# Both mixers of the first block reordered: first table load, second weight tile, filler products, tile rests and masks

## The reference

```python
def mla_mixer(h, w_dq, q_norm, w_uq, w_dkv, kv_norm, w_ukv, q_gain, k_gain, w_o):
    cq = rms_norm(h @ w_dq, q_norm)
    q = (cq @ w_uq).reshape(b, s, MLA_HEADS, MLA_QK)
    dkv = h @ w_dkv
    ckv = rms_norm(dkv[..., :MLA_KV_RANK], kv_norm)
    k_rope = jnp.broadcast_to(dkv[..., None, MLA_KV_RANK:], (b, s, MLA_HEADS, MLA_ROPE))
    kv = (ckv @ w_ukv).reshape(b, s, MLA_HEADS, MLA_NOPE + MLA_V)
    ...
    q = rms_norm(q, q_gain)
    k = rms_norm(k, k_gain)
    ...
    o = chunk_causal_attention(q, k, v)
    return o.reshape(b, s, MLA_HEADS * MLA_V) @ w_o

def mlstm_mixer(h, w_in, w_if, b_if, head_norm, w_o):
    q, k, v, o_pre = jnp.split(h @ w_in, [hq, 2 * hq, 2 * hq + hv], axis=-1)
    ...
        dmat = bcum[..., :, None] - bcum[..., None, :] + li[..., None, :]
        dmat = jnp.where(causal, dmat, -jnp.inf)
        m_t = jnp.maximum(inter, jnp.max(dmat, axis=-1))
        w_intra = jnp.exp(dmat - m_t[..., None])
        qk = jnp.einsum('bhtd,bhsd->bhts', qc, kc) * w_intra
        ...
        hc = num / jnp.maximum(jnp.abs(den), jnp.exp(-m_t))[..., None]
```

## Time and profile before

| | us |
|---|---|
| time, median of three runs | 1621.61 |
| the three runs | 1624.91, 1621.61, 1619.29 |
| profiled execution, time | 1625.26 |
| its span, first to last instruction | 1623.4 |
| TensorE busy | 1585.5 (98%) |
| VectorE busy | 1076.5 (66%) |
| ScalarE busy | 863.8 (53%) |
| GpSimd busy | 151.3 (9%) |
| mean granted TensorE clock | 0.986 of full |

### The profile page before, as it was taken

One profiled execution on the slowest core, in us unless ns is written; L12 is line 12 of the kernel. 1 busy time (PEld: TensorE's weight loads), 2 busy tenths in 40 slices (PEclk: granted clock), 3 DMA queues, 4 the chain that ended last, 5 costly groups with the idle time before them and its releaser, 6 DMA issues.

```text
span 1623.4 us, 33219 instructions
## 1 busy us (share of the span) xinstructions
PE 1585.5 (98%) x11604; PEld 1492.1 (92%) x11604; DVE 1076.5 (66%) x1817; ACT 863.8 (53%) x1381; POOL 151.3 (9%) x133
## 2 busy tenths in 40 slices
PE   7899999999999999999999999999999999999999
PEld 6789998877999889999899999889999878999997
DVE  6668766645677666666787766678566755686665
ACT  5576554444765545445545545556455546664443
POOL 1650000075200000000000000000000032200000
PEclk8899999989999999999999999999999999999999
DMA  6226556543565565555655655556555871065564
GB/s 227 73 56 192 193 182 193 183 155 117 168 190 186 182 196 188 185 183 192 204 188 182 197 189 188 188 181 207 179 190 193 216 198 65 2 195 189 186 195 142
DMA packets 80766, 280.72 MB, mean 173 GB/s; under 512 B 8880, under 2 KB 12464, under 8 KB 80688
## 3 DMA queue, kind: packets, MB, share of 16 engines
q1 hardware_dynamic: 76800, 274.78, 52.5%
q10 hardware_dynamic: 3888, 4.85, 1.6%
HBM read 278.03 MB, written 1.57 MB: 172 GB/s over the span
## 4 chain that ended last, share of the span: by engine, by line
PE 90%; DVE 5%; ACT 2%; DMA 2%; issue 1%; DVEq 0%; ACTq 0%; SPq 0%
PE psum L1692 17%; PE psum L1693 17%; PE psum L1694 17%; PE psum L1684 16%; PE psum L1685 8%; PE psum L1820 2%; PE psum L1822 2%; PE psum L1821 2%; DMA raw<-tiles 1%; DVE w_lo L1006 1%; PE psum L2095 1%; PE psum L2046 1%; PE psum L1994 1%; ACT w_hi L538 1%; DVE w1c_all L1570 0%
## 5 line engine op out<-in xcount | busy, mean ns | idle before, releaser
L538 ACT ACTIVATE w_hi<-raw 128x1024 fp32r<-128x1024 f32 x518 | 546.8, 1057 | 447.9 <-PE psum L1694 263.2
L1006 DVE TENSOR_TENSOR w_lo<-raw,w_hi 128x1024 fp32r<-128x1024 f32 x472 | 577.0, 1223 | 219.6 <-ACT w_hi L538 219.2
L1692 PE MATMUL psum<-xs,w_hi 128*128 128x256 f32 x1928 | 541.6, 281 | 8.5 <-DVE w_lo L1006 5.8
L1694 PE MATMUL psum<-xs,w_lo 128*128 128x256 f32 x1928 | 539.9, 280 | 0.0
L1693 PE MATMUL psum<-xs,w_hi 128*128 128x256 f32 x1928 | 538.9, 279 | 0.0
L1684 PE MATMUL psum<-hs,w_hi 128*128 128x512 f32 x1216 | 421.9, 390 | 0.0
L1692 PEld LDWEIGHTS psum<-xs,w_hi 128*128 128x128 f32 x1928 | 363.5, 189 | 9.5 <-DVE w_lo L1006 6.2
L1693 PEld LDWEIGHTS psum<-xs,w_hi 128*128 128x128 f32 x1928 | 363.5, 189 | 0.3
L1694 PEld LDWEIGHTS psum<-xs,w_lo 128*128 128x128 f32 x1928 | 363.4, 188 | 0.0
L1685 PE MATMUL psum<-hs,w_lo 128*128 128x256 f32 x1216 | 342.9, 282 | 0.0
L1684 PEld LDWEIGHTS psum<-hs,w_hi 128*128 128x128 f32 x1216 | 228.3, 188 | 47.7
(11 more groups left out here) (285 smaller groups left out, 1571.5 us busy)
## 6 DMA issues: line engine op xcount, KB each, us to landing
raw<-tiles SPq DMA_DIRECT2D x518, 512.0 KB, 4.2
bias<-bias_dram ACTq DMA_DIRECT2D x8, 256.0 KB, 8.4
x<-x_in SPq DMA_DIRECT2D x4, 256.0 KB, 5.1
w1c_all<-w1c_k ACTq DMA_DIRECT2D x4, 256.0 KB, 4.2
w1c_all<-w1c_v ACTq DMA_DIRECT2D x4, 256.0 KB, 5.3
y_out<-x SPq DMA_DIRECT2D x8, 128.0 KB, 3.4
con<-consts SPq DMA_DIRECT2D x1, 771.0 KB, 8.9
bias_dram<-bias_row ACTq DMA_DIRECT2D x1, 512.0 KB, 7.2
```

Source lines behind the costliest of these rows:

```text
L538: act.activation(w_hi[s][:, :], raw[s][:, :], ACT.Copy).then_inc(hi_ready, 1)
L1006: dve.tensor_tensor(w_lo[s][:, :], raw[s][:, :], hi_of(w_hi[s][:, :]), ALU.subtract).then_inc(lo_ready, 1)
L1692: pe.matmul(out, w_hi[s][:, c:c + P], x_hi, start=first, stop=False)
L1694: return pe.matmul(out, w_lo[s][:, c:c + P], x_hi, start=False, stop=last)
```

## The change

Start: ScalarE loads its table ahead of its first waits; tile 1 is split, and its rest made, directly behind x, tile 2 behind four squares (five sums on VectorE); TensorE runs 24 fillers.

First mixer: GpSimd's stretch begins two tiles later, and VectorE makes the rests of those two. The copy of `kr` moves ahead of the last three rests of the compressed inputs. VectorE adds the squares of the compressed inputs chunk by chunk, so that four one-column products take the place of ten; a new semaphore, `cq_added`, says so. The product of the gains, the bias row and the mask rows come ahead of the norm's reciprocal. Reads and head sums change places. The values get a 65th column of ones for each head (`v3`), whose product is the row sum, so ScalarE no longer sums; outputs of both halves are scaled by one instruction. Eight fillers stand before the first probabilities are turned, ScalarE loads the exponentials' table behind the root, and splits the last tile behind the first turned probabilities.

Matrix-memory mixer: GpSimd's stretch begins ten tiles later, and VectorE makes those rests behind each read. The running sums stand behind the fifth q/k tile (`decays`), maxima and their differences behind the sixth (`stabilizers`); turning and scores come one or two steps earlier in `mv`. A mask of 0 and -1e30 (`m_mask`) takes part in the exponents instead of two multiplications. The denominator is formed by two instructions instead of three.

```diff
...
@@ -250,7 +251,7 @@
-        POOL_TILES = [(TILE0["uq"], TILE0["wo_a"] + RING), (TILE0["mgate"] + RING, TILE0["wo_m"] + RING), (TILE0["ngate"] + RING, TILE0["wo_n"] + RING)]
+        POOL_TILES = [(TILE0["uq"] + 2, TILE0["wo_a"] + RING), (TILE0["mv"] + RING, TILE0["wo_m"] + RING), (TILE0["ngate"] + RING, TILE0["wo_n"] + RING)]
...
@@ -687,7 +690,6 @@
                 split(tv)
-                split(tv + 1)
@@ -698,7 +700,7 @@
-                                       bias=nmx[u][:, tb:tb + 1], accum_out=rsum[u][:, tb:tb + 1]).then_inc(a_exp, 1)
+                                       bias=nmx[u][:, tb:tb + 1]).then_inc(a_exp, 1)
@@ -710,10 +712,12 @@
                 act.activation(std[:, 0:2 * H], ss[:, 0:2 * H], ACT.Sqrt, bias=eps[:, 0:1], scale=1.0 / QK).then_inc(head_std, 1)
+                act.preload_act_table(ACT.Exp)
                 turned(0, 2)
...
                 probs_turned(0, 0)
+                split(tv + 1)
                 heads_loop(act, lambda i, u: ahead(turned, i, u, 3), lambda i, u: ahead(probs_turned, i, u, 1),
...
@@ -932,6 +936,7 @@
+            act.preload_act_table(ACT.Copy)
@@ -939,9 +944,10 @@
                     split(0)
+            split(1)
             for k in range(KD):
-                if k in (3, 6):
-                    split(k // 3)
+                if k == 4:
+                    split(2)
                 act.activation(ASQ[:, k * S:(k + 1) * S], x[:, k * S:(k + 1) * S], ACT.Square).then_inc(sq_ready, 1)
@@ -1033,13 +1039,15 @@
-            def plain(name, outs, dst, p=slice(None), lo=False):
+            def plain(name, outs, dst, p=slice(None), lo=False, between=None):
...
+                    if between and o in between:
+                        between[o]()
@@ -1207,16 +1215,25 @@
+                        narrow("kr", ROPE)
...
-                narrow("kr", ROPE)
-                norm("cq")
+                dve.wait_ge(sq_ready, SQ0["cq"] + 1)
+                first, second = (ASQ[:, 0:2 * KQ * S].rearrange("p (k s) -> p k s", s=KQ * S)[:, :, n * S:(n + 1) * S] for n in range(2))
+                then(dve.tensor_tensor(first, first, second, ALU.add))
+                dve.tensor_tensor(ASQ[:, 0:S], ASQ[:, 0:S], ASQ[:, 2 * S:3 * S], ALU.add).then_inc(cq_added, 1)
+                for t in range(TILE0["uq"], TILE0["uq"] + 2):
+                    take_lo(t)
+                dve.wait_ge(loaded, 16 * 3)
+                then(dve.tensor_tensor(gq[:, 0:NOPE], gq[:, 0:NOPE], gk[:, 0:NOPE], ALU.mult))
...
-                dve.wait_ge(loaded, 16 * 3)
...
+                dve.memset(v3[:, :, VD:], 1.0).then_inc(a_mask, 1)
+                norm("cq")
...
@@ -1241,9 +1262,9 @@
-                then(dve.tensor_tensor(gq[:, 0:NOPE], gq[:, 0:NOPE], gk[:, 0:NOPE], ALU.mult))
+                head_sums(0)
...
-                for n in range(3):
+                for n in (1, 2):
@@ -1254,13 +1275,13 @@
-                up_kv("uq", q_tok, 2)
...
+                up_kv("uq", q_tok, 2)
...
-                up_kv("uv", v_tok, 1)
...
+                up_kv("uv", v_tok, 1)
@@ -1278,15 +1299,16 @@
+                o3 = o_tok.rearrange("p (t c) -> p t c", t=TB)
...
-                    dve.wait_ge(a_exp, i * 8 + 2 * (u + 1))
-                    then(dve.reciprocal(rinv[u], rsum[u]))
...
-                    for tb in range(TB):
-                        col = tb * P + u % 2 * VD
-                        ins = dve.tensor_scalar(at(o_tok, i * (4 * VD) + (tb * H * VD + u * VD), VD), bank(6 + u % 2, col, col + VD),
-                                                rinv[u][:, tb:tb + 1], None, ALU.mult)
-                    ins.then_inc(a_o, 1)
+                    pv = bank(6 + u % 2, 0, 2 * P).rearrange("p (t c) -> p t c", t=TB)
+                    then(dve.reciprocal(rinv[u].unsqueeze(2), pv[:, :, VD:VD + 1]))
+                    first = i * (4 * VD) + u * VD
+                    o = o3[:, :, first:first + VD] if isinstance(i, int) else o3[:, :, bass.ds(first, VD)]
+                    dve.tensor_tensor(o, pv[:, :, 0:VD], rinv[u].unsqueeze(2).to_broadcast([P, TB, VD]), ALU.mult).then_inc(a_o, 1)
@@ -1306,23 +1328,32 @@
+                causal = const("causal", 0, P)
+                then(dve.memset(m_mask, 0.0))
+                dve.tensor_scalar(m_mask[:, 0:P], causal, -1.0, 1.0e30, ALU.add, ALU.mult)
...
+                    take_lo(TILE0["mgate"] + o + RING)
...
-                plain("mqk", 8, lambda o: m_qk[:, o * S:(o + 1) * S])
...
-                dve.wait_ge(m_tanh, 4)
-                then(dve.tensor_tensor_scan(m_nb, m_one, m_tf, 0.0, ALU.mult, ALU.add))
-                then(dve.scalar_tensor_tensor(out=m_a, in0=m_ti, scalar=GATE_CAP, in1=m_nb, op0=ALU.mult, op1=ALU.add))
-                then(dve.tensor_tensor_scan(m_g, m_a, m_a, 0.0, ALU.max, ALU.max))
-                dve.tensor_scalar(m_ng, m_g, -1.0, None, ALU.mult)
-                dve.tensor_tensor(m_nm, m_nb, m_g, ALU.subtract).then_inc(m_rows, 1)
-                causal = const("causal", 0, P)
+                def decays():
+                    dve.wait_ge(m_tanh, 4)
+                    then(dve.tensor_tensor_scan(m_nb, m_one, m_tf, 0.0, ALU.mult, ALU.add))
+                    then(dve.scalar_tensor_tensor(out=m_a, in0=m_ti, scalar=GATE_CAP, in1=m_nb, op0=ALU.mult, op1=ALU.add))
+                def stabilizers():
+                    then(dve.tensor_tensor_scan(m_g, m_a, m_a, 0.0, ALU.max, ALU.max))
+                    dve.tensor_scalar(m_ng, m_g, -1.0, None, ALU.mult)
+                    dve.tensor_tensor(m_nm, m_nb, m_g, ALU.subtract).then_inc(m_rows, 1)
+                plain("mqk", 8, lambda o: m_qk[:, o * S:(o + 1) * S], lo=True, between={4: decays, 5: stabilizers})
@@ -1333,16 +1364,15 @@
-                    dve.tensor_scalar(m_w[h][:, 0:S], bank(b, 0, S), m_col[:, h:h + 1], 0.0, ALU.add, ALU.min)
-                    dve.tensor_scalar(m_w[h][:, S:S + P], bank(b, P, S), m_col[:, MH + h:MH + h + 1], 0.0, ALU.add, ALU.min)\
-                       .then_inc(m_logw, 1)
+                    dve.scalar_tensor_tensor(out=m_w[h][:, 0:S], in0=bank(b, 0, S), scalar=m_col[:, h:h + 1], in1=m_mask,
+                                             op0=ALU.add, op1=ALU.min)
+                    dve.scalar_tensor_tensor(out=m_w[h][:, S:S + P], in0=bank(b, P, S), scalar=m_col[:, MH + h:MH + h + 1],
+                                             in1=m_mask[:, 0:P], op0=ALU.add, op1=ALU.min).then_inc(m_logw, 1)
...
-                    dve.tensor_tensor(w[:, 0:P], w[:, 0:P], causal, ALU.mult)
-                    then(dve.tensor_tensor(w[:, S:S + P], w[:, S:S + P], causal, ALU.mult))
@@ -1361,11 +1391,10 @@
-                    then(dve.tensor_scalar(m_nd[h], den, -1.0, None, ALU.mult))
-                    then(dve.tensor_tensor(m_dn[h], den, m_nd[h], ALU.max))
...
-                    then(dve.tensor_tensor(m_dn[h], m_dn[h], floor, ALU.max))
+                    then(dve.scalar_tensor_tensor(out=m_nd[h], in0=den, scalar=-1.0, in1=floor, op0=ALU.mult, op1=ALU.max))
+                    then(dve.scalar_tensor_tensor(out=m_dn[h], in0=den, scalar=1.0, in1=m_nd[h], op0=ALU.mult, op1=ALU.max))
@@ -1634,13 +1663,14 @@
                     take_lo(0)
+            take_lo(1)
             clear_sums("mix_0")
...
                 dve.tensor_tensor(ssq[:, :], ssq[:, :], ASQ[:, k * S:(k + 1) * S], ALU.add).then_inc(ssq_ready, 1)
-                if k in (3, 6):
-                    take_lo(k // 3)
+                if k == 4:
+                    take_lo(2)
             take_lo(3)
@@ -1696,12 +1726,11 @@
-                    pe.wait_ge(sq_ready, SQ0["cq"] + 1)
+                    pe.wait_ge(cq_added, 1)
...
-                        for k in range(KQ + KKV):
-                            col, first, last = (4, 0, KQ - 1) if k < KQ else (6, KQ, KQ + KKV - 1)
+                        for k, col in ((0, 4), (KQ, 6)):
...
-                                            start=k == first, stop=k == last)
+                                            start=True, stop=True)
@@ -1897,19 +1926,20 @@
-                    v = [at(v_tok, i * (4 * VD) + (tb * H * VD + u // 2 * P), P) for tb in range(TB)]
-                    pe.matmul(bank(b, 0, P), pT[:, 0:P], v[0], start=True, stop=True)
-                    pe.matmul(bank(b, P, 2 * P), pT[:, P:2 * P], v[0], start=True, stop=False)
-                    pe.matmul(bank(b, P, 2 * P), pT[:, 2 * P:3 * P], v[1], start=False, stop=True).then_inc(a_pv, 1)
+                    v = [at(v_tok, i * (4 * (VD + 1)) + (tb * H + u) * (VD + 1), VD + 1) for tb in range(TB)]
+                    pe.matmul(bank(b, 0, VD + 1), pT[:, 0:P], v[0], start=True, stop=True)
+                    pe.matmul(bank(b, P, P + VD + 1), pT[:, P:2 * P], v[0], start=True, stop=False)
+                    pe.matmul(bank(b, P, P + VD + 1), pT[:, 2 * P:3 * P], v[1], start=False, stop=True).then_inc(a_pv, 1)
...
-                pe.wait_ge(a_mask, 2)
+                pe.wait_ge(a_mask, 3)
...
+                warm(8, 6)
@@ -1955,8 +1985,8 @@
```

(6 more changed lines are left out.)

23 lines of the change are left out of this document (15 added, 8 removed).

## The result

The changed kernel takes **1595.94 us** (median of four runs, 1594.70 to 1598.29); the kernel before, beside it, 1622.09 (four runs, 1619.29 to 1624.91). The ratio is 0.984, with a 95% interval of 0.9819 to 0.9862: 26.2 us, 1.6%. The prediction was 1598, range 1590 to 1606.

What follows compares the result with a forecast made beforehand. TensorE runs products back to back, so only its waits and low-clock stretches can give time: 1.7 + 10.4 + 1.2 + 0.2 + 11.2 = 24.7 us. From 1625.26, less 3.65 to the median, 1596.9; predicted 1598, range 1590 to 1606.

Steps and rivals of the forecast that it cites:

- step 3: Head loop's start: first probabilities ready 1.6 us sooner, eight new fillers end 1.2 earlier; gain 1.2 us, bounds 0 to 1.6.
- the loop: Head loop: TensorE at 2.11 us a head without pause hides dropped work; only the tail gains, 0.2 us.
- Step 1: Start: earlier table load and sooner second tile, less a clock fall in a new wait; gain 1.7 us.
- "3.2 us" for the orders: Start: without a slow clock the third tile starts at 18.8 for 22.0, 3.2 us sooner.
- Step 2: First compressed part to first query product: VectorE sets that product, at +9.1 for +19.5 after kr's end; gain 10.4 us.
- rival (a): First mixer: GpSimd's tile runs first and catches VectorE's second copy; first query product at +11.5, 4.7 us lost, 1603; chance 0.18.
- "nothing" for the narrower products: Head loop: value products of 65 columns gain nothing, since a one-column pass already costs 0.11 us, like a 128-column one.
- 3 us for the loop: Head loop, rival: narrower value products pay by columns, some 3 us over 96 passes, 1595; chance 0.05.
- rival (b): Whole kernel: waits go but the clock falls elsewhere as often; only 13.6 us gained, 1608; chance 0.08.
- Step 4: Matrix-memory mixer: stabilizer wait 3.8 and its clock 4.0, denominator wait 1.9 and its clock 1.5; gain 11.2 us.
- (d): Start: early table load is repeated at first use, leaving only a shorter second wait; 1600, chance 0.04.
- (e): Mixer's q/k stage: VectorE becomes the bound, each of ten tiles waits at low clock; slower, 1632, chance 0.03.

Runs made afterwards that it cites:

- the second profile: The changed kernel, unaltered, run and profiled again beside the follow-up experiments: median 1596.82 us, ratio 0.9863 to the kernel before; profiled execution 1595.13 us.

## Why the prediction was right, and where it was not

**The whole.** 24.7 us forecast for what the change touches, 22.6 and 24.9 in the two profiles. The other 3.7 between profile and median that I took off are borne out by the traces: the rest of the program, the same code in thirteen of the fourteen traces, takes 1171.3 to 1179.9 us, and the profile of before is the longest of them. ScalarE there waits 2.46 us for a weight tile, and the clock falls for 6.83 and 3.41 us:

```profile
1315.48 1.06 ACT L538 ACTIVATE w_hi<-raw 128x1024 fp32r<-128x1024 f32 x1 [2.46 <-DMA raw<-tiles]
```

That the second profile gives 24.9 for 24.7 is in part luck: the clock held at its start, 1.2 us more than forecast, and step 3 and the loop gave 0.6 us less each.

**Step 1** has the right size (1.7 forecast, 1.5 measured, 2.9 in the second profile) for the wrong reason. Its times hold one by one: first product 8.74 for 8.65, second wait 0.8 for 1.0, wait for the sums 2.4 for 2.5, last add 17.99 for 18.2, third tile 18.94 for 18.8, one slow stretch of 3.4. The step that failed is "3.2 us" for the orders. With the old orders the third tile starts at 19.2 where the clock falls early, and at 21.9 where it falls late. So in the traces the order gives 0.2, and the rest is how often and where the clock falls. The old start lost 0, 2.8 and 2.8 us to it in three traces, the new one without fillers 0 to 2.8 in six. The 24 fillers end at 8.98 by the timeline, not 8.3, and so run up to the first product; in the second profile that comes at 9.05, 0.5 behind the rest of its tile (8.55). It costs nothing, since TensorE then waits for the second tile all the same.

**Step 2** holds as worked out: sums ready at +2.7 for +2.9, first query product at +9.0 for +9.1, wait 0.9 for 1.2, 10.4 us. In nine of the ten traces that share its code the first query product comes at 8.98 or 8.99; the odd one is the sums behind the third tile, at 11.93. The second copy started 0.56 ahead of GpSimd, not 0.2, and rival (a) was real: moving the sums of the first norm elsewhere brought it about. It came at +11.9 for the +11.5 of (a), and cost 5.4 for 4.7. That VectorE set the product is shown by the copies moved out of its way; TensorE's own path then gives +7.9, for the +7.7 of the prediction. The rule that the Trainium skill gives for the shared port (SBUF — State Buffer, section "SBUF: two separate sides"), that whichever starts first has it for the whole instruction, is borne out: there the second copy was due some 0.2 us behind GpSimd's start and waited for the whole tile of 2.4.

**Step 3**: 1.2 forecast, 0.7 measured, inside its bounds. I had the reads' order lose nothing in front; it loses 0.7 there and wins 1.1 behind.

**The loop and its tail** were mis-sized. The one-column row, from which I took "nothing" for the narrower products, was no measure for them: they gave 0.05 us in a plain head and 0.4 in the loop. By the figures of the Trainium skill (TensorE: Matmul & The Clock Gate, section "Back-to-back issue gap") the prediction had 3 us for the loop; the runs have 0.4, an eighth. From the first turned probabilities to the last the loop fell from 32.27 us to 31.39; the 0.5 that the columns leave belongs to work that I had called hidden (ScalarE's accumulator reads, VectorE's fused output) or to the tail, and no run separates these. What I had not seen is the fall at the end of the loop: it costs 0.9 to 2.3 us by the stretches from the first turned probabilities to the end of `wo_a` (60.3 to 61.7, for 59.4 with fillers), and turned +0.2 into -1.4 and -0.4. It is a small case of rival (b), "it falls elsewhere": here with waits of at most 0.6 us, where I had said that each fall lies at a wait of over 2.

**Step 4**: 11.4 for 11.2. The rows end 3.3 us ahead of TensorE, not 1.8, TensorE waits 0.2 us for the second numerators, as forecast, and the ten rests cause no wait:

```profile
369.43 0.70 PE L1982 MATMUL psum<-arena 128*128 128x257 f32 x2 [0.16 <-DVE arena L1400]
```

Of its terms the waits are firm. The 5.5 us of clock was an execution's draw: putting the mixer back brought 3.2.

Rivals (d) and (e) are excluded: the table is loaded once at 0.74 with no second load before the first split, and no q/k tile is waited for.

## What to carry to other kernels

Where GpSimd works on SBUF data, count VectorE's operations with two SBUF inputs, an SBUF copy or a `tensor_scalar` from SBUF at GpSimd's duration (here 1.9 to 2.7 us for steps of 0.2 to 0.7), not their own. Moving GpSimd's two tiles away gave 3.1 us, moving VectorE's copies into its idle time 1.1. A gain from a slow clock in one trace is a draw: read the same stretch in several profiles before it is credited to an edit. Where TensorE must stand still, filler products ahead of the wait (ahead of the first one that blocks, not behind it) kept the clock here; after shortening small products, look whether the work that is left still keeps it.

## What the hardware showed that I had not expected

- The clock fell behind two or three waits of 0.3 to 0.6 us within 3 us (in the first profile after the change, from 94.8 to 97.7), in seven of seven traces, and not when value products of 128 columns instead of 65 stood between waits of the same size.
- It also fell with no wait ahead. In six of the fourteen traces it falls for 3.41 us some 10 us ahead of the wait of 2.2 us in the attention of the second block, and again at that wait; in the other eight it does not fall ahead of that wait, with the same code of this block up to there. In the kernel with the old order of reads, TensorE works through 1312 to 1321.3 at full clock without a gap, and then gets half of it. Of the 56 products there 16 have 30 columns and 16 have 64 rows:

```profile
1312.00:1321.30 9.30, 9.30 (x56) 1.00 0.32 113
1321.36:1324.77 3.41, 3.41 (x17) 0.50 0.00 0
```

  What brings this on stays open; no run here was aimed at it.
- A fall can cost nothing: the one from 10.98 to 14.39 lay ahead of a wait for a weight tile, which became shorter by as much.
